# Attention scores and values of a Hymba block on the whole array: zero-padded keys and values, products of 256 columns

## The reference

```python
def sliding_window_attention(q, k, v, sinks, slopes):
    ...
    kb, vb = band(k), band(v)          # each chunk's 128 keys: the previous chunk and its own
    scores = jnp.einsum('bcqkgd,bcskd->bckgqs', qc, kb) * (ATT_HEAD_DIM ** -0.5)
    bias = -slopes.reshape(ATT_KV_HEADS, ATT_GROUP, 1, 1) * dist
    scores = jnp.where(valid, scores + bias, -jnp.inf)
    probs = jax.nn.softmax(jnp.concatenate([scores, sink], axis=-1), axis=-1)[..., :-1]
    out = jnp.einsum('bckgqs,bcskd->bcqkgd', probs, vb)
```

## Time and profile before

| | |
|---|---|
| Median of 3 runs | 992.05 us (991.84 to 992.35) |
| The profiled execution | 992.37 us |
| Its span, first to last instruction | 990.6 us |
| TensorE busy | 983.1 us (99%) |
| VectorE, ScalarE, GpSimd busy | 652.9, 422.9, 667.2 us |
| Attention stage, by the units | about 191 to 292 us |
| Chain that ended last | TensorE 90%, VectorE 3%, DMA 2% |

### The profile page before, as it was taken

How to read it: one execution, slowest core, us unless ns; L and a number is a source line. 1 busy time by engine, 2 the same in 40 slices (tenths; PEclk the granted TensorE clock), 3 DMA queues, 4 the chain that set the end, 5 groups by cost and what they waited for, 6 DMA issues and landing times.

```text
span 990.6 us, 13176 instructions
## 1 busy us (share of the span) xinstructions
PE 983.1 (99%) x4816; PEld 814.8 (82%) x4816; DVE 652.9 (66%) x808; ACT 422.9 (43%) x868; POOL 667.2 (67%) x529
## 2 busy tenths in 40 slices
PE   9999999999999999999999999999999999999998
PEld 7898888878888888888888888888888888888887
DVE  5596345569843696958757485866748577674485
ACT  5542155467622665525243342524334352433440
POOL 0164466626784328978868777877877787887792
PEclk9999999999999999999999999999999999999999
DMA  8634435541321002121121121122112112112213
GB/s 294 211 85 81 110 79 138 138 164 33 108 65 32 22 22 85 54 64 43 43 86 44 43 73 55 43 60 68 43 43 85 43 43 80 48 42 62 78 58 134
DMA packets 103592, 76.87 MB, mean 78 GB/s; under 512 B 30696, under 2 KB 83944, under 8 KB 103528
## 3 DMA queue, kind: packets, MB, share of 16 engines
q1 hardware_dynamic: 102168, 75.00, 25.2%
q10 hardware_dynamic: 1360, 1.02, 0.4%
HBM read 68.15 MB, written 7.36 MB: 76 GB/s over the span
## 4 chain that ended last, share of the span: by engine, by line
PE 90%; DVE 3%; DMA 2%; ACT 1%; SPq 1%; issue 1%; POOL 0%; ACTq 0%; DVEq 0%
PE banks L878 29%; PE banks L880 28%; PE banks L879 28%; DMA x_in<-in_x 1%; PE banks L1065 1%; PE banks L891 1%; PE banks L968 1%; ACT prob L1582 1%; PE banks L1040 1%; PE banks L980 0%; DMA rstd_b<-rstd_rows 0%; PE banks L1027 0%; DMA rstd_rows<-rpadT 0%; PE banks L990 0%; PE banks L953 0%
## 5 line engine op out<-in xcount | busy, mean ns | idle before, releaser
L808 POOL TENSOR_TENSOR wr_lo<-wr_raw,wr_hi 128x512 fp32r<-128x512 f32 x231 | 319.0, 1412 | 27.1 <-ACT wr_hi L1394 21.9
L802 POOL TENSOR_TENSOR wr_raw<-wr_raw,wr_raw 128x512 f32<-128x512 f32 x132 | 193.6, 1471 | 132.3 <-PE banks L880 72.7
L878 PE MATMUL banks<-hf_hi,wr_hi 128*128 128x512 f32 x616 | 240.2, 390 | 0.0
L879 PE MATMUL banks<-hf_lo,wr_hi 128*128 128x512 f32 x616 | 239.8, 389 | 0.0
L880 PE MATMUL banks<-hf_hi,wr_lo 128*128 128x512 f32 x616 | 239.8, 389 | 0.0
L1394 ACT ACTIVATE wr_hi<-wr_raw 128x512 fp32r<-128x512 f32 x231 | 136.6, 625 | 165.0 <-POOL wr_raw L802 106.0
L2246 DVE TENSOR_TENSOR x<-banks,x 128x1024 f32<-128x1024 f32 x138 | 168.8, 1225 | 51.5 <-PE banks L880 35.2
L878 PE MATMUL banks<-w_hi,actT_hi 128*128 128x512 f32 (+1 forms) x384 | 147.1, 383 | 0.9 <-POOL w_lo L739 0.8
L880 PE MATMUL banks<-w_hi,actT_lo 128*128 128x512 f32 (+1 forms) x384 | 143.3, 373 | 0.0
L879 PE MATMUL banks<-w_lo,actT_hi 128*128 128x512 f32 (+1 forms) x384 | 143.0, 372 | 0.0
L878 PEld LDWEIGHTS banks<-hf_hi,wr_hi 128*128 128x128 f32 x616 | 115.7, 188 | 24.4 <-issue 0.4
(11 more groups left out here) (206 smaller groups left out, 1201.5 us busy)
## 6 DMA issues: line engine op xcount, KB each, us to landing
wr_raw<-in_w_up SPq DMA_DIRECT2D x46, 256.0 KB, 3.2
wr_raw<-in_w_gate SPq DMA_DIRECT2D x44, 256.0 KB, 3.4
wr_raw<-in_w_down SPq DMA_DIRECT2D x44, 256.0 KB, 3.1
w_raw<-in_w_in SPq DMA_DIRECT2D x32, 256.0 KB, 3.6
x_in<-in_x SPq DMA_DIRECT2D x4, 1024.0 KB, 13.1
w_raw<-in_w_out SPq DMA_DIRECT2D x16, 256.0 KB, 2.7
x<-in_x SPq DMA_DIRECT2D x8, 512.0 KB, 6.1
out<-x SPq DMA_DIRECT2D x16, 256.0 KB, 2.1
```

Of the source, the lines that this page charges most:

```text
L802: nc.gpsimd.tensor_tensor(wr_raw[slot(q, f)][:, :], wr_raw[slot(q, a)][:, :], wr_raw[slot(q, b)][:, :], ALU.subtract).then_inc(wsum, 1)
L808: nc.gpsimd.tensor_tensor(wr_lo[s][:, :], wr_raw[s][:, :], wr_hi[s][:, :].bitcast(F32), ALU.subtract).then_inc(wf_lo, 1)
L878: nc.tensor.matmul(ps, x_hi, wh, start=first, stop=False, skip_group_check=more)
L879: nc.tensor.matmul(ps, x_hi, wl, start=False, stop=False, skip_group_check=more)
```

## The change

Keys and values are padded with zeros, so that one product on the whole array does the work of a pair. `kTz` holds for each key head a copy of the keys in which the other head's 64 partitions are zero; a score product has all 128 rows, moves both key heads' 128 keys at once (256 columns) and writes one chunk's bank: 4 products in place of 8, with the semaphores `s_c0` and `s_c1` after each chunk. `v_prev` and `v_cur` hold a zero block between the two heads' values, so that a window of 128 columns is one head's values beside zeros; a value product moves 256 columns of probabilities and the two key heads are summed in PSUM: 4 in place of 8. The result's features come in another order of heads, so the first half of W_out is loaded by heads, each slice in two transfers of 64 partitions, and g_attn_out in two small ones. The values reach `v_prev` and `v_cur` by six transfers on SP's queue behind the bias, in place of two on ScalarE's. VectorE writes the zeros and the second key copy behind the first tile's normalised queries; before, it wrote small zeros after the key projection. `pT` moves onto the place of `kvs`, so its first copies wait for the six transfers; `bias` moves onto the place of `g_row`, whose load moves behind the last scores.

```diff
@@ -144,6 +145,7 @@
         nm_b0, _ = place("nm_b0", [P, N], at=base[0] - 4 * D)
         nm_b1, _ = place("nm_b1", [P, N], at=base[0] - 2 * D)
         nm_b = [nm_b0, nm_b1]
+        bias, _ = place("bias", [P, 2, N], at=base[0] - 4 * D)
         stat, _ = place("stat", [P, T])
         rstd, _ = place("rstd", [P, T])
...
@@ -207,9 +209,12 @@
 
         V = g_end
         kvs, e = place("kvs", [P, T, NKV], at=V)
-        v_prev, e = place("v_prev", [P, T, KV * HD], at=e)
-        w1_raw, _ = place("w1_raw", [P, K, NKV], at=V + 4 * T * NKV)
-        kT, v_end = place("kT", [P, CHUNK + S], at=e)
+        pT0, pe_ = place("pT0", [P, 8, P], at=V)
+        pT1, pe_ = place("pT1", [P, 8, P], at=pe_)
+        assert pe_ <= e
+        w1_raw, _ = place("w1_raw", [P, K, NKV], at=e)
+        kTz, v_end = place("kTz", [P, KV, CHUNK + S], at=e)
+        kT0, kT1 = kTz[:, 0, :], kTz[:, 1, :]
         h2buf0, e = place("h2buf0", [P, D], at=V)
         h2buf1, e = place("h2buf1", [P, D], at=e)
...
@@ -229,16 +234,16 @@
         qkT, e = place("qkT", [P, 4, S], at=E)
         mvx, e = place("mvx", [P, T, MH, DV + 1], at=e)
         msq, _ = place("msq", [P, MH * DV], BF16, at=e)
-        bias, e = place("bias", [P, 2, N], at=E)
-        qT0, e = place("qT0", [P, 4, P], at=e)
+        qT0, e = place("qT0", [P, 4, P], at=E)
         qT1, e = place("qT1", [P, 4, P], at=e)
         prob0, e = place("prob0", [P, 8, P], at=e)
         prob1, e = place("prob1", [P, 8, P], at=e)
-        pT0, e = place("pT0", [P, 8, P], at=e)
         qn, e = place("qn", [P, 4, KV, HD], at=e)
         sqb, e = place("sqb", [P, N], at=e)
         pq, e = place("pq", [P, N], at=e)
-        pT1, e = place("pT1", [P, 8, P], at=e)
+        v_prev, e = place("v_prev", [P, T, 3 * HD], at=e)
+        v_cur, e = place("v_cur", [P, T, 3 * HD], at=e)
+        vz = [v_prev, v_cur]
         qT, prob, pT = [qT0, qT1], [prob0, prob1], [pT0, pT1]
 
...
@@ -425,12 +430,15 @@
 
             g, k = 1 + n // K, n % K
             if g == 1:
-                return [((0, 8), w_in_k[k, :, GATES:GATES + 8]),
-                        ((8, NKV), w_in_k[k, :, AK:AK + 2 * KV * HD])]
+                return [((0, P), (0, 8), w_in_k[k, :, GATES:GATES + 8]),
+                        ((0, P), (8, NKV), w_in_k[k, :, AK:AK + 2 * KV * HD])]
             if g < 5:
                 c = {2: MV, 3: MO, 4: AQ}[g]
-                return [((0, N), w_in_k[k, :, c:c + N])]
-            return [((0, N), w_out_k[k, :, (g - 5) * N:(g - 4) * N])]
+                return [((0, P), (0, N), w_in_k[k, :, c:c + N])]
+            n_ = slice((g - 5) * N, (g - 4) * N)
+            if k < 4:
+                return [((kv * HD, (kv + 1) * HD), (0, N), w_out_h[kv * 4 + k, :, n_]) for kv in range(KV)]
+            return [((0, P), (0, N), w_out_k[k, :, n_])]
 
         NS = 6 * K
...
@@ -571,9 +579,11 @@
                     sp.dma_start(tri[:, :], consts[:, C_TRI:C_TRI + P]).then_inc(par_s, 16)
                     sp.dma_start(prow[G_CONV:G_CONV + 16, :],
                                  conv_qk.rearrange("a i (f p) -> (a i f) p", p=P)).then_inc(par_s, 16)
-                    for i, g in enumerate((g_att, g_ml)):
-                        rows = slice(G_OUT + 4 * i, G_OUT + 4 * i + 4)
-                        sp.dma_start(prow[rows, :], g.rearrange("a (k p) -> (a k) p", p=P)).then_inc(par_s, 16)
+                    for kv in range(KV):
+                        sp.dma_start(prow[G_OUT:G_OUT + 4, kv * HD:(kv + 1) * HD],
+                                     g_att.rearrange("a (v e d) -> v (a e) d", v=KV, d=HD)[kv]).then_inc(par_s, 16)
+                    sp.dma_start(prow[G_OUT + 4:G_OUT + 8, :],
+                                 g_ml.rearrange("a (k p) -> (a k) p", p=P)).then_inc(par_s, 16)
                     for half in range(2):
                         sp.dma_start(prow[G_K:G_K + 1, half * HD:(half + 1) * HD], k_gain).then_inc(par_s, 16)
...
-                for (a, b), src in slice_source(n):
-                    sp.dma_start(w_raw[:, n % RAW, a:b], src).then_inc(raw_s[n % RAW], 16)
+                for (p0, p1), (a, b), src in slice_source(n):
+                    sp.dma_start(w_raw[p0:p1, n % RAW, a:b], src).then_inc(raw_s[n % RAW], 16)
                 if 2 <= n - 3 * K < T - 1:
                     load_keys(n - 3 * K)
...
@@ -668,9 +678,19 @@
                     for i, c in enumerate((C_FIRST, C_BIAS)):
                         sp.dma_start(bias[:, i, :], consts[:, c:c + N]).then_inc(late_s, 16)
 
+                    for i in range(KV):
+                        v = kvs[:, :, 2 * MH + (KV + i) * HD:2 * MH + (KV + i + 1) * HD]
+                        to = slice(2 * i * HD, (2 * i + 1) * HD)
+                        sp.dma_start(v_cur[:, :, to], v).then_inc(v_moved, 16)
+                        sp.dma_start(v_prev[CHUNK:P, :, to], v[0:CHUNK, :, :]).then_inc(v_moved, 16)
+                        sp.dma_start(v_prev[0:CHUNK, 1:T, to], v[CHUNK:P, 0:T - 1, :]).then_inc(v_moved, 16)
+
                     sp.wait_ge(ssb_done, T)
                     for t in range(4):
                         sp.dma_start(x1[:, t, :], x_t[t]).then_inc(x1_s[0], 16)
+                if n == 5 * K + 5:
+
+                    sp.wait_ge(s_evac, T)
                     sp.dma_start(g_row[:, :], g_ffn[0:1, :].to_broadcast([P, D])).then_inc(gf_s, 16)
 
...
@@ -1016,18 +1036,17 @@
                 pe.wait_ge(qT_ready, t + 1)
                 if t >= 1:
                     pe.wait_ge(s_evac, t)
+                if t == 0:
+                    pe.wait_ge(v_zero, 1)
                 q = qT[t % 2]
-                for c2 in range(2):
+                for c2, done in ((0, s_c0), (1, s_c1)):
 
                     start = t * P + c2 * CHUNK
                     for b in range(2):
-                        o = (c2 * 2 + b) * P
-                        for kv, done in ((0, s_kv0), (1, s_kv1)):
-                            rows = slice(kv * HD, (kv + 1) * HD)
-                            last = nc.tensor.matmul(bank[4 + kv][:, o:o + P], q[rows, 2 * b + c2, :],
-                                                    kT[rows, start:start + P], start=True, stop=True)
-                            if (c2, b) == (1, 1):
-                                last.then_inc(done, 1)
+                        o = bank[4 + c2][:, :].rearrange("p (v m n) -> p m v n", v=KV, m=2)[:, b]
+                        last = nc.tensor.matmul(o, q[:, 2 * b + c2, :], kTz[:, :, start:start + P],
+                                                start=b == 0, stop=b == 1, skip_group_check=True)
+                    last.then_inc(done, 1)
 
             def att_prob_transposes(t):
...
@@ -1047,23 +1066,18 @@
                 pe.wait_ge(pTd, t + 1)
                 if t == 0:
                     pe.wait_ge(v_zero, 1)
-                    pe.wait_ge(v_moved, 16 * 2)
+                    pe.wait_ge(v_moved, 16 * 6)
                 pe.wait_ge(qT_ready, min(t + 4, T))
                 if t >= 1:
                     pe.wait_ge(mixa_ready, t)
+                o = bank[2][:, :].rearrange("p (e c n) -> p c e n", e=4, c=2)
                 for c2 in range(2):
                     for kv in range(KV):
-                        if c2 == 0:
-                            v = v_prev[:, t, kv * HD:(kv + 1) * HD]
-                        else:
-                            v = kvs[:, t, 2 * MH + (KV + kv) * HD:2 * MH + (KV + kv + 1) * HD]
-                        for i2 in range(2):
-                            rows = slice(i2 * HD, (i2 + 1) * HD)
-                            b0 = kv * 4 + c2 * 2
-                            rhs = pT[t % 2][:, b0:b0 + 2, i2 * CHUNK:(i2 + 1) * CHUNK]
-                            o = bank[2][rows, kv * 2 * P:(kv + 1) * 2 * P].rearrange("p (b n) -> p b n", b=2)
-                            last = nc.tensor.matmul(o[:, :, c2 * CHUNK:(c2 + 1) * CHUNK], v, rhs,
-                                                    start=True, stop=True)
+                        b0 = kv * 4 + c2 * 2
+                        rhs = pT[t % 2][:, b0:b0 + 2, :].rearrange("p b n -> p (b n)")
+                        last = nc.tensor.matmul(o[:, c2], vz[c2][:, t, kv * HD:kv * HD + P], rhs,
+                                                start=kv == 0 and c2 == 0, stop=kv == 1 and c2 == 1,
+                                                skip_group_check=True)
                 last.then_inc(pv_done, 1)
 
...
@@ -1491,13 +1505,6 @@
                     nc.scalar.activation(qkT[:, f, :], qkT[:, f, :], ACT.Silu).then_inc(qk_ready, 1)
                 if U == SILU_AT[-1]:
                     nc.scalar.preload_act_table_set("natural_log_exp_and_others")
-                if U == 2 * T:
-
-                    vcols = slice(2 * MH + KV * HD, 2 * MH + 2 * KV * HD)
-                    act.wait_ge(acc_free[0], T // 2)
-                    act.wait_ge(acc_free[1], T // 2)
-                    act.dma_start(v_prev[CHUNK:P, :, :], kvs[0:CHUNK, :, vcols]).then_inc(v_moved, 16)
```

(33 more changed lines are left out.)

13 lines of the change are left out of this document (8 added, 5 removed).

## The result

| | before | changed |
|---|---|---|
| Median | 992.05 us (991.84 to 992.35) | 999.78 us (999.27 to 1000.22) |
| Profiled execution | 992.37 us, span 990.6 | 999.42 us, span 997.7 |
| Ratio | | 1.0078 [1.0060, 1.0095] |

Slower by 7.7 us. The forecast was 1001.3, with 997.5 to 1005. The page of the changed kernel: engine totals, the granted clock, the shares of the chain.

A forecast was written before the change was run, and what follows sets the result against it. TensorE was taken to bound the kernel. On the profiled 992.37 us: +0.6 up to the first values, +8.7 from there, +0.1 start, -0.2 closing gaps, together +9.2, 1001.6; less 0.3 for the median, 1001.3 us; range 997.5 to 1005.

The forecast's parts named there:

- The bound: TensorE bounds the attention stage, 99.24 us of work in 101 us; its longer work adds to the end except before the first values.
- A pair runs in the time of one record: In the attention products, two records on the array's two halves run in the time of one whole-array record, 0.109 us.
- The pitch of a 256-column record: Each whole-array record of the new score and value products takes 0.220 us, between 0.217 and 0.227.
- rival 1: Score and value products: a 256-column record costs little more than a 128-column one, 0.11 us; 990.1 us, faster; chance 4%.
- Rival 3: Score and value products: a 256-column record takes 0.198 us and the stall at 203 us stays away; 998.5 us; chance 12%.
- The mode changes: TensorE loses about 0.1 us at each of three whole/half-array changes in a tile; their removal alone gives back 0.3 us.
- Up to the first values: VectorE's 4.4 us block makes TensorE wait 0.6 us near 203 us; the first three tiles' extra score work is hidden; +0.6.
- Rival 2: VectorE's zeros before the first values last 7.5 us instead of 4.4, a 3.7 us stall at 203 us; 1004.4; chance 15%.
- The start: One more small load at the kernel's start delays SP by 0.4 us; 0 to 0.4 us, taken as 0.1.
- Transfers: Six value copies on SP's queue land before 211 us, ahead of their first reader after 218 us; no cost in the sum.
- rival 4: The six value copies take 20 us instead of 6, land after 218 us and hold the first values 4 us; 1005; 4%.
- Rival 5: TensorE's extra work in the attention is hidden altogether; 992 us, chance 2%.

## Why the prediction was right, and where its sum was off

**The bound.** Right. From the first values on nearly each microsecond of TensorE's work came to the end, and the stages behind 292 us kept their length (+7.14 throughout). TensorE's share of the chain that ended last stayed at 90%.

**A pair runs in the time of one record.** Right, and shown twice: undone in the change (9.36 us a tile with both as pairs) and destroyed without the change (998.39 with the pairs apart). The reading from starts and from the chain was the one that carried: the records' mean length rose from 285 to 379 ns, by a third, while the pitch of a record on the whole array doubled, 0.109 to 0.216 us.

**The pitch of a 256-column record.** 0.216 us instead of 0.220, just below my lower bound of 0.217. Eight records each for the values of 8 tiles and the scores of 5 make 104 from the first values on, and this 0.4 us. The price by the column was right, so rival 1 (0.11 us) is out. Rival 3's 0.198 is out too, and so is the Trainium skill's spacing behind it (TensorE: Matmul & The Clock Gate, Back-to-back issue gap): the trace doesn't agree with the 0.196 us that I estimated from its sustained spacing. Against this rival I had also read the two warm-up records of 512 columns by their length, 2.08 us, as four times those of 128. By their starts, which I had said to go by, it is 0.99 to 1.01 us against 0.213, over four times. The conclusion holds, but 0.213 is twice the later 0.109, so these rows are no measure of the pitch in the attention.

**The mode changes.** This is the term that was mis-sized. I put 0.1 us on each of three changes in a tile. Read record by record in the tile from 229.04, a change costs about 0.1 us to the first record behind it, and the next record comes late as well: by 0.10 us in the scores, 0.05 in the values, 0.10 in the sum of squares. Together that is 0.55 us a tile, and the changed kernel has none of it. I counted what lies between the last transpose and the sum of squares, and wrote that the saved mode changes were in it. The last of these 0.1 us lies behind that: from the sum of squares to the unit it is 0.14 us instead of 0.24, in each of the seven tiles where it stands behind values, 0.7 us. In tiles 6 and 7 values come without scores ahead of them, and there the change into them is saved too, 0.09 us each: those tiles lost 0.51 us, where I had put 0.73. Per settled tile I forecast +1.31 and the trace has +1.18. The Trainium skill's page TensorEngine Tiling (Array Packing), under Tiling Modes, Key Properties, says that a mode change drains TensorE; the runs are in keeping with a cost at each change, but don't show that a drain is its cause.

**The gap at 254 us.** A gap of TensorE behind the transposed probabilities, before the unit at 254.65, closed by 0.34 us; in the kernel before, TensorE's weight load waited 0.35 us there for VectorE's `qn`. I had 0.2 for all such gaps. From the first values on my sum was 8.7 - 0.2 = 8.5 and the trace has 7.18. Pitch 0.4, mode changes 0.7 + 0.2 and this gap 0.14 add up to 1.4, where 1.3 lies between them. Of the 0.1 too many, most is the first value record behind the wait, which takes 0.29 us to the next instead of 0.216 (221.50 to 221.79).

**Up to the first values.** Forecast +0.6, measured 0.68 and 0.47 in the two profiles of the changed kernel and about 0 with three operations moved. The block took 4.5 us where I had 4.4, but the parts differed: the copy of 64 x 1088 took 0.72 us and not 1.3, and 1.0 until the next operation began, the zeros 0.96 as worked out, the last operation 0.22 and not 0.11, as it writes 64 x 192 and not the 64 x 64 I had, and the handing over between the operations 0.7 instead of 0.1. That the sum came out was luck: what was too much in the copy was missing there. The room before the first values took up all extra score work of the first three tiles, as forecast. Rival 2 (a stall of 3.7 us, 1004.4) didn't happen; the run with the block doubled shows what it would have been, and that it would have been dearer than I priced, since the clock falls with such a wait.

**The start.** +0.1 forecast, -0.70 measured in the first profile, -0.25 in the second, +0.16 with the load alone: chance, and as large as the difference between the profiled shift of 7.1 and the medians' 7.7.

**Transfers.** Right as to the time: the run with both parts paired carries all of them and is at 1.0007. They had landed by about 209 us, where I had 211, and no wait of TensorE in the attention names a DMA, so rival 4 is out. Rival 5 (hidden) is out by the time. The chance of faster was written as 0.03, where half of case 1 is 0.02.

## What to carry to other kernels

Two products on different halves of the array's rows or columns ran side by side here. Filling the array with zeros to make one product of them then gains nothing and loses what the wider product takes: count records at their pitch, read from starts, not lengths. Padding costs nothing only where the engine has idle time to fill: the same extra work was free ahead of a wait of 1.6 us and cost its full length behind it. (Halves that have no partner would be another case; no run here has them.) And a wait put on the busy engine can cost more than its length: here one of 4.7 us cost 1.2 more, as the clock fell with it.

## What the hardware showed that I had not expected

- TensorE overlaps records on its two halves that are not neighbours in the program: the other half's began about four records ahead of their turn (232.04 us in the timeline of the pairs taken apart), so they started before records listed ahead of them. That an engine runs in program order, as I wrote of the kernel before, thus doesn't hold for the starts on TensorE's two halves. In groups of four records nearly the full gain stays (1.19 and 1.07 us against 1.09 and 1.03).
- A mode change costs about 0.1 us to the first record behind it, in both directions: 0.20 in place of 0.11 from a transpose to a score pair of 128 columns, 0.31 in place of 0.216 from the last 256-column score record to the value pairs (230.17 + 7 x 0.216 = 231.68, to 231.99). The record after that is late too, by 0.05 to 0.10: this is the 0.24 in place of 0.14 from the sum of squares behind the values to the unit.
- With a wait of 4.7 us the granted clock fell to 0.50, already before the wait ended; after waits of 0.5 and 1.6 us in this stage it stayed at 1.00.
- VectorE copied 64 x 1088 float32 within SBUF in 0.72 us, faster than it wrote as many zeros (0.96). So it was in seven of the eight such copies of these runs; the first in the run with the zeros twice took 1.04.
